# The last stage of a decoder layer: three of eight shift additions go from VectorE to GpSimd, and the square root's table is loaded ahead

## The reference

```python
    x = x + gt2[:, None, :] * ffn
    mod_f = c_act @ w_ada_final + b_ada_final
    sh_f, sc_f = jnp.split(mod_f, 2, axis=-1)
    return modulate(rmsnorm(x, norm_f_g), sh_f, sc_f, dt)
    # rmsnorm(x, g) = x * rsqrt(mean(x*x) + 1e-6) * g
    # modulate(h, shift, scale) = h * (1 + scale) + shift
```

## Time and profile before

| | us |
|---|---|
| median of 3 runs | 1054.54 |
| the runs | 1052.35 to 1054.55 |
| the profiled execution's own time | 1054.91 |
| its span | 1053.1 |
| TensorE's granted clock, mean share of full | 0.98 |
| sum of tile 0 to 3 on TensorE in the last stage begins | 1013.34 |
| last shift ends | 1049.99 |

### The profile page before, as it was taken

How to read it: one execution, slowest core, us unless ns; L and a number is a source line. 1 busy time by engine, 2 the same in 40 slices (tenths; PEclk the granted TensorE clock), 3 DMA queues, 4 the chain that set the end, 5 groups by cost and what they waited for, 6 DMA issues and landing times.

```text
span 1053.1 us, 15470 instructions
## 1 busy us (share of the span) xinstructions
PE 979.8 (93%) x5658; PEld 768.8 (73%) x5658; DVE 798.3 (76%) x1484; ACT 529.1 (50%) x929; POOL 109.4 (10%) x151
## 2 busy tenths in 40 slices
PE   3899988999999999999999999799999999999996
PEld 3668768987897998989988888366666666666642
DVE  8767758944894895967775768888888887777828
ACT  4545432653265465554653333266656656565532
POOL 0200101000100001010000000112211221212100
PEclk9699989999999999999999999899999999999998
DMA  9733423330333225230185434469999999999275
GB/s 365 240 96 119 136 91 91 112 100 22 109 93 101 66 72 164 62 101 1 42 321 185 180 139 182 175 251 367 371 364 366 374 363 359 361 354 347 98 308 210
DMA packets 81033, 206.78 MB, mean 196 GB/s; under 512 B 11878, under 2 KB 40630, under 8 KB 72780
## 3 DMA queue, kind: packets, MB, share of 16 engines
q1 hardware_dynamic: 59232, 156.25, 41.2%
q0 software_dynamic: 15120, 43.72, 13.0%
q10 hardware_dynamic: 6620, 6.00, 1.7%
HBM read 189.61 MB, written 24.71 MB: 204 GB/s over the span
## 4 chain that ended last, share of the span: by engine, by line
PE 60%; DVE 20%; DMA 11%; ACT 4%; issue 4%; SPq 0%; ACTq 0%; DVEq 0%
PE PS L1946 11%; PE PS L1948 10%; PE PS L1947 10%; DMA WGU<-in_w_exp_up 7%; PE PS L2227 4%; DMA AR<-in_w_ada 3%; PE PS L2013 3%; PE PS L2235 3%; PE PS L2234 3%; PE PS L2233 3%; DVE ACC L1253 3%; DVE AT L1427 3%; DVE WL L1318 2%; PE PS L2218 2%; PE PS L2337 1%
## 5 line engine op out<-in xcount | busy, mean ns | idle before, releaser
L1946 PE MATMUL PS<-WH,HT 128*128 128x256 f32 x512 | 147.1, 287 | 1.3 <-ACT GVH L919 1.3
L1947 PE MATMUL PS<-WL,HT 128*128 128x256 f32 x512 | 145.0, 283 | 0.0
L1948 PE MATMUL PS<-WH,HL 128*128 128x256 f32 x512 | 144.9, 283 | 0.0
L1783 DVE TENSOR_TENSOR WGL<-WGU,WGH 128x1024 fp32r<-128x1024 f32 x96 | 116.9, 1220 | 20.1 <-ACT WGH L1161 18.8
L1427 DVE COPY_PREDICATED AT<-MASK,PS 128x64 f32<-128x64 uint8 x320 | 72.7, 227 | 65.9 <-PE PS L2024 47.0
L1161 ACT ACTIVATE WGH<-WGU 128x1024 fp32r<-128x1024 f32 x96 | 98.6, 1064 | 40.5 <-DMA WGU<-in_w_exp_up 32.9
L1946 PEld LDWEIGHTS PS<-WH,HT 128*128 128x128 f32 x512 | 98.4, 192 | 4.0 <-issue 4.0
L1947 PEld LDWEIGHTS PS<-WL,HT 128*128 128x128 f32 x512 | 98.5, 192 | 0.0
L1948 PEld LDWEIGHTS PS<-WH,HL 128*128 128x128 f32 x512 | 98.3, 192 | 0.0
L2233 PE MATMUL PS<-WGH,XGTH 128*96 128x512 f32 x192 | 88.4, 461 | 0.0
L1821 DVE TENSOR_TENSOR WDL<-WDN,WDH 128x2048 fp32r<-128x2048 f32 x32 | 73.4, 2292 | 17.8 <-ACT WDH L1171 17.7
(11 more groups left out here) (349 smaller groups left out, 2248.2 us busy)
## 6 DMA issues: line engine op xcount, KB each, us to landing
WGU<-in_w_exp_gate SPq DMA_DIRECT2D x32, 1024.0 KB, 12.5
WGU<-in_w_exp_up SPq DMA_DIRECT2D x32, 1024.0 KB, 18.6
WDN<-in_w_exp_down SPq DMA_DIRECT2D x32, 1024.0 KB, 14.0
AR<-in_w_ada POOLq DMA_DIRECT2D x32, 512.0 KB, 4.5
WF<-in_w_in SPq DMA_DIRECT2D x28, 512.0 KB, 5.4
AST<-in_w_ada SPq DMA_DIRECT2D x16, 512.0 KB, 9.1
AR<-in_w_ada_final POOLq DMA_DIRECT2D x16, 512.0 KB, 4.4
YG<-expert_rows SPq DMA_DIRECT2D x8, 1024.0 KB, 13.3
```

The lines of the kernel that those rows point to most:

```text
L1783: V.tensor_tensor(WGL[s][:, :, ks, :], WGU[s][:, :, ks, :], WGH[(NCH * s + c) % 4][:].bitcast(F32), ALU.subtract).then_inc(wgl_ready, 1)
L1946: MM(ps, wh, xh, start=first, stop=False)
L1947: MM(ps, wh, xl, start=False, stop=False)
L1948: return MM(ps, wl, xh, start=False, stop=last)
```

## The change

The shift of tiles 0, 2 and 4 (`SHIFT_ON_POOL`) is added by GpSimd, with the same operands; the other five stay with VectorE. GpSimd waits for `out_scaled`, and a new semaphore `pool_out` tells SyncE when each of the three is done. SyncE still stores in the order of the tiles. On ScalarE one square root of a constant 128x1 tile (`ONESF`, into the unused `TOCK`) stands ahead of the loop over the tiles. Two semaphores that nothing used are dropped.

```diff
+        SHIFT_ON_POOL = (0, 2, 4)
+        SHIFT_ON_DVE = [t for t in range(NT) if t not in SHIFT_ON_POOL]
...
-        idxc = sem("idxc")
...
-        idxs = sem("idxs")
...
+        pool_out = sem("pool_out")
...
             for t in range(NT):
-                sp.wait_ge(out_ready, t + 1)
+                if t in SHIFT_ON_POOL:
+                    sp.wait_ge(pool_out, SHIFT_ON_POOL.index(t) + 1)
+                else:
+                    sp.wait_ge(out_ready, SHIFT_ON_DVE.index(t) + 1)
                 sp.dma_start(out_rows[:, t, :], OUTT[:, t % 4, :]).then_inc(out_st[t % 4], 16)
...
             pool.sem_inc(extras_done, 1)
+            pool.wait_ge(rows_in, 32)
+            for t in SHIFT_ON_POOL:
+                pool.wait_ge(out_scaled, t + 1)
+                nc.gpsimd.tensor_tensor(OUTT[:, t % 4, :], OUTT[:, t % 4, :], SHF[:], ALU.add).then_inc(pool_out, 1)
...
+            A(TOCK[:], ONESF[:], ACT.Sqrt)
             for t in range(NT):
...
-                shifted(t)
+                if t in SHIFT_ON_DVE:
+                    shifted(t)
```

## The result

The changed kernel took 1056.01 us (median of 18 runs, 1054.68 to 1060.08), the kernel before 1054.23 (median of 18, 1052.15 to 1056.68): a ratio of 1.002, 95% interval 1.0013 to 1.0027. It is slower by 0.2%, some 2 us, where 1.2 us less was forecast.

The account below looks back on a forecast made before the run. VectorE's rounds in the last stage were taken as the bound; 0 for the table, 0 for the shift of tile 0 and 2 x (-0.62) gave -1.24 us, so 1053.3 us from 1054.54, range 1052.2 to 1057.0.

Parts of the forecast that it names:

- What bounds the kernel: Last stage: VectorE's own work sets the end, 4.24 us a round, with 2.3 us of room before the next bound.
- The sum: Last stage: 0 for table and tile 0, -0.62 us for each of two rounds, -1.24 us if VectorE loses nothing.
- The first rival: VectorE's second inverse instruction, with two SBUF operands, waits for GpSimd's add: 1056.7 us (1055.2 to 1058.3), chance 0.35.
- The rival's own price: VectorE's wait for GpSimd's add in two rounds: D - 0.68 each, +2.2 us in sum at D = 2.4.
- D: Time of GpSimd's add of one shift, taken as 2.4 us; VectorE's waiting decides from 1.3 us on.
- two bounds: Estimates of GpSimd's add over 1024 columns: 1.66 us with one input, 3.2 if the second doubles the column cost.
- the formula: Net change if VectorE waits for GpSimd in two rounds: 2 x (D - 0.68) - 1.24 us.
- The first tile's wait is absorbed by TensorE: VectorE's wait beside GpSimd's shift of tile 0 costs nothing, as the add of tile 3 waits for TensorE anyway.
- The stores: SyncE's in-order stores: a GpSimd shift of tile 4 of up to 4.8 us delays none; buffers are free in time.
- The range: Whole time 1052.2 to 1057.0 us, meant to take in most of the case where VectorE waits for GpSimd.
- the forecast's own range: Whole time if the forecast alone holds: 1052.3 to 1054.2 us, chance 0.50.
- The first sign of error: Rounds 1, 3 and 5: a second inverse instruction that starts late or lasts 1 to 2 us, ending with GpSimd's add.

Follow-up runs that it names:

- e1: Kernel before with only the early square root (table load) added, all shifts on VectorE: 1054.82 us, ratio 1.0002.
- e4: Changed kernel with GpSimd's three adds replaced by a memset of the same buffers: 1054.71 us (one run).
- e2: Changed kernel without the early square root, shifts of tiles 0, 2 and 4 still on GpSimd: 1056.96 us, ratio 1.0022.
- e6: Changed kernel with the shift of tile 6 also on GpSimd and a one-operand inverse in tiles 1, 3, 5 and 7: 1058.35 us, ratio 1.0034.
- e12: Kernel before with GpSimd only waiting for the scale of tile 6 before it ends: 1059.51 us, ratio 1.0043.
- e8: Changed kernel, but GpSimd begins the shift of a tile only when the next tile's inverse is done: 1055.79 us, ratio 1.0007.

## Why the prediction was wrong

- **What bounds the kernel**: right. VectorE's rounds set the end, the table alone is worth nothing (e1), the round without a shift is bound by VectorE, ScalarE, VectorE at 3.6 us (forecast 3.62; 3.56 and 3.55 in e4). It gives back 0.68 us and not 0.62, since ScalarE's hand-over, taken as 0.10 from tile 0, is 0.04 here (1030.68 to 1030.72).
- **The sum**: its condition failed. "If GpSimd's work costs VectorE nothing" stood under the -1.24 us, and it costs 1.53 us (1.75 - 0.22) in each of rounds 3 and 5: 2 x (1.53 - 0.68) = +1.70 on the stage. The first rival was what happened, and I gave it 0.35 against 0.50 for the forecast. No row shown of before bore on that choice. The Trainium skill (SBUF — State Buffer, "Who interferes with whom") did: a VectorE instruction with two SBUF inputs contends with a GpSimd instruction that reads SBUF, not with one that only writes it. The trace agrees with it, 1.75 us instead of 0.22, and 0.22 beside a memset.
- **The rival's own price**: D was put at 2.4 us and measured at 2.34 to 2.35. That it came so near is luck: the middle of two bounds was taken for want of a row, and both bounds were off (a copy takes 1.04 instead of 1.66, and the second input more than doubles it). The wait was D - 0.68 = 1.66 by the formula and 1.53 in the trace: the waiting instruction came 0.61 into GpSimd's add and not 0.68, and it ended with that add and not a whole 0.22 behind it. With that and the 0.68 above the stage lost 1.70 instead of the formula's 2.08 at that D.
- **"The first tile's wait is absorbed by TensorE"**: right in the changed kernel (0.88 us of the second inverse instruction in round 1, and the add of tile 3 still waited 0.94). It holds because of the early table; without it 0.4 us get through (e2).
- **The stores**: right, none was late. GpSimd's shift of tile 4 ended at 1041.96, before VectorE's of tile 5 did (1045.89). But the end of GpSimd's program was not looked at. A drain that no part of the prediction names ended 2.9 us ahead of SyncE's; here it cost nothing, but the shift of tile 6 would have run into it (e6).
- **The range** held the time (1056.01 in 1052.2 to 1057.0) because it took in the rival; the forecast's own range did not. The first sign of error that was named, a second inverse instruction of 1 to 2 us that ends with GpSimd's add, is the one that the trace shows.

## What to carry to other kernels

Before giving GpSimd work on SBUF, list what VectorE does in those microseconds and look for instructions with two SBUF tensor operands, the 128x1 ones too: a tiny one on the critical chain can last until the GpSimd instruction ends (1.75 us instead of 0.22 here). Give that factor as a per-partition scalar instead, or let the overlap fall on instructions that read PSUM. And look at what closes a program: work that GpSimd is given near the end can put its drain on the path (+4 us in e6).

## What the runs showed of the hardware that had not been expected

- GpSimd's closing drain takes 10.11 us by itself (e12) and in every profile taken it lasted 10.1 to 10.2 us beyond the instruction or wait that came last; VectorE's ended within 0.04 us of its last instruction (1.26 us from the start of a 1.23 us shift). GpSimd issues DMAs earlier in every kernel here; whether its drain is as long without them was not tried.
- The overlap isn't lost in full. VectorE's blocked instruction ends less than its usual duration behind the end of GpSimd's: counted back by that duration, it starts 0.2 us before GpSimd's end in three cases: beside the add (1030.91 + 1.75 - 0.22 = 1032.44 against 1032.65), beside the copy (1030.82 against 1031.03), and the scale in e8 (1032.43 + 2.36 - 1.28 = 1033.51 against 1033.70). For the blocked shifts in e8 and e6 it is 0.15 and 0.14 us. Whether VectorE is let go that much early, or has done the first part of its instruction before it waits, these rows don't tell.
- Not all that GpSimd does holds VectorE up. In the trace of before, VectorE's 96 instructions WGL<-WGU,WGH (128x1024, two SBUF tensors, L1783) all take 1.21 to 1.23 us, though GpSimd is issuing an indirect DMA beside some of them (one at 741.53 beside GpSimd's of 0.94 us at 741.42).
- GpSimd on 128x1024 float32: 2.35 us for an add of two operands, 1.04 for a copy, 0.95 for a memset. The one-input bound that had been worked out from a 128x128 select (1.66 us) was too high by 0.6 for a copy.
